# First output projection: groups 0 to 2 with tokens as output rows and a turn through DRAM, sums of squares moved into the next projection

## The reference, cut to what matters

```python
def pool_mixer(h, w_in, w_grp, scale, w_out):
    ...
    y = jnp.einsum('btgc,gcd->btgd', pooled, w_grp).reshape(B, T, BRANCH_W) * scale
    return (y * jax.nn.silu(g)) @ w_out          # the first output projection
...
    x = x + gate * y
    return rms_norm(x) * final_norm_g            # end of the first block
...
def gated_deltanet(h, w_in, ...):                # after another rms_norm of h
    proj = h @ w_in.astype(h.dtype)              # the projection called G_A below
    qkv = proj[..., :3 * A_INNER]
    a_in = proj[..., 4 * A_INNER:4 * A_INNER + A_HEADS]
    b_in = proj[..., 4 * A_INNER + A_HEADS:]
```

## Time and profile before

| what | value |
|---|---|
| median of 3 runs | 1334.66 us (1333.32 to 1334.88) |
| profiled execution, its own time | 1334.82 us |
| span of the profile | 1332.7 us |
| TensorE matmul busy | 1326.0 us (99%) |
| VectorE busy | 960.7 us (72%) |
| ScalarE busy | 732.5 us (55%) |
| DMA, mean over the span | 255 GB/s |
| first output projection begins | 247.55 us |
| first group of `G_A` begins, next group begins | 338.34 us, 365.21 us |

### The profile page before, as it was taken

How to read it: one execution, slowest core, us unless ns; L and a number is a source line. 1 busy time by engine, 2 the same in 40 slices (tenths; PEclk the granted TensorE clock), 3 DMA queues, 4 the chain that set the end, 5 groups by cost and what they waited for, 6 DMA issues and landing times.

```text
span 1332.7 us, 18992 instructions
## 1 busy us (share of the span) xinstructions
PE 1326.0 (99%) x6963; PEld 1109.1 (83%) x6963; DVE 960.7 (72%) x1279; ACT 732.5 (55%) x1091; POOL 196.8 (15%) x313
## 2 busy tenths in 40 slices
PE   9999999999999999999999999999999999999999
PEld 5445999988888888888888988888888888888887
DVE  4558999988779898999676668746666566666552
ACT  2213435456766657556688775465655646565431
POOL 0000012100001000032122200002234234232000
PEclk9999999999999999999999999999999999999999
DMA  9999989885676776599866676656879889789662
GB/s 383 394 416 371 353 345 408 299 279 181 202 248 207 239 226 222 182 294 293 222 181 198 201 236 224 194 186 205 260 236 270 261 271 283 217 278 262 179 197 83
DMA packets 90354, 339.36 MB, mean 255 GB/s; under 512 B 12368, under 2 KB 12768, under 8 KB 85792
## 3 DMA queue, kind: packets, MB, share of 16 engines
q1 hardware_dynamic: 67392, 261.30, 57.7%
q0 software_dynamic: 22880, 76.94, 19.0%
HBM read 310.91 MB, written 29.38 MB: 255 GB/s over the span
## 4 chain that ended last, share of the span: by engine, by line
PE 81%; DMA 12%; DVE 5%; issue 1%; ACT 1%; SPq 0%; POOL 0%; DVEq 0%; POOLq 0%
PE acc L905 19%; PE acc L848 14%; PE acc L849 14%; PE acc L850 14%; PE acc L909 10%; DMA mod_ring<-mod_w 7%; DMA raw<-weights 5%; PE misc L1174 2%; DVE w_lo L1903 1%; PE misc L905 1%; PE misc L1164 1%; DVE mod_ring L1873 1%; PE misc L1065 1%; DVE mod_late L1873 1%; DVE gate_ring L1873 1%
## 5 line engine op out<-in xcount | busy, mean ns | idle before, releaser
L1903 DVE TENSOR_TENSOR w_lo<-raw,w_hi 128x1024 fp32r<-128x1024 f32 x392 | 471.5, 1221 | 178.7 <-ACT w_hi L1339 173.1
L1339 ACT ACTIVATE w_hi<-raw 128x1024 fp32r<-128x1024 f32 x392 | 405.4, 1054 | 321.6 <-DMA raw<-weights 234.7
L848 PE MATMUL acc<-w_hi,b_op 128*128 128x512 f32 x704 | 277.1, 394 | 0.0
L849 PE MATMUL acc<-w_lo,b_op 128*128 128x512 f32 x704 | 274.3, 390 | 0.0
L850 PE MATMUL acc<-w_hi,b_op 128*128 128x512 f32 x704 | 274.3, 390 | 0.0
L905 PE MATMUL acc<-b_op,w_hi 128*128 128x512 f32 x640 | 162.1, 395 | 0.0
L850 PEld LDWEIGHTS acc<-w_hi,b_op 128*128 128x128 f32 x704 | 132.2, 188 | 27.5
L848 PEld LDWEIGHTS acc<-w_hi,b_op 128*128 128x128 f32 x704 | 132.4, 188 | 26.3
L849 PEld LDWEIGHTS acc<-w_lo,b_op 128*128 128x128 f32 x704 | 132.4, 188 | 26.1
L905 PEld LDWEIGHTS acc<-b_op,w_hi 128*128 128x128 f32 x640 | 115.2, 189 | 21.0 <-issue 0.2
L905 PE MATMUL acc<-a_op,w_hi 128*128 128x512 f32 x448 | 113.1, 394 | 0.3 <-DVE a_op L1913 0.3
(11 more groups left out here) (314 smaller groups left out, 2012.8 us busy)
## 6 DMA issues: line engine op xcount, KB each, us to landing
raw<-weights SPq DMA_DIRECT2D x392, 512.0 KB, 5.1
mod_ring<-mod_w SPq DMA_DIRECT2D x26, 1024.0 KB, 14.4
u_ring<-weights SPq DMA_DIRECT2D x32, 512.0 KB, 14.6
gate_ring<-weights POOLq DMA_DIRECT2D x30, 512.0 KB, 8.3
mod_late<-mod_w SPq DMA_DIRECT2D x6, 1024.0 KB, 6.4
head_d<-head POOLq DMA_DIRECT2D x32, 128.0 KB, 4.3
t<-head_d POOLq DMA_DIRECT2D x32, 128.0 KB, 5.9
z_d<-z POOLq DMA_DIRECT2D x28, 128.0 KB, 4.8
```

Of the source, the lines that this page charges most:

```text
L848: nc.tensor.matmul(to, xh[:, t], wh, start=kt == 0, stop=False)
L849: nc.tensor.matmul(to, xh[:, t], wl, start=False, stop=False)
L1339: nc.scalar.activation(w_hi[:, m.c % HL_SLOTS], raw[:, q.c % RAW_SLOTS], ACT.Copy).then_inc(own.up(s_hi), 1)
L1903: nc.vector.tensor_tensor(w_lo[:, slot], raw[:, q.c % RAW_SLOTS], w_hi[:, slot].bitcast(F32), ALU.subtract).then_inc(own.up(s_lo), 1)
```

## The change

Groups 0 to 2 of the first output projection are computed by token into three pairs of PSUM banks. ScalarE copies each to SBUF (`out_by_token`), VectorE transposes its blocks (`out_turned`), GpSimd turns it through DRAM, and VectorE adds the result, times the gate, to the residual in one step per group (`gated`, four instructions). Group 3 stays `joined`, in the plain order. VectorE's work there is written out anew: group 3's second half is added before the squares of group 2 are summed. `early_sums` moves from group 3 into the first group of `G_A`, behind its slab at position 3, and `last_sums` from position 4 to 5. Weights of the three groups are laid out on the host in the other slab form. Numbers of turns that other stages wait for are shifted by three.

```diff
-TURNS = tuple([("va", v) for v in range(4)] + [("za", 0), ("za", 1), ("za", 2)] +
+TURNS = tuple([("y", j) for j in range(3)] + [("va", v) for v in range(4)] + [("za", 0), ("za", 1), ("za", 2)] +
...
+        y_part = [vo[:, k:k + 4].rearrange("p k t -> p (k t)") for k in (8, 4, 8)]
+        y_32 = at("y_32", [P, 4 * T], F32, vo_at + 12288)
...
-            for j in (2, 3):
-                pool.wait_ge(s_gate, 29 + j)
-                x_again(j)
...
+            def out_turned(j):
+
+                n, through = turn_of("y", j), head_d[0] if j == 1 else z_d
+                pool.wait_ge(s_head_32, n)
+                to_dram(y_32[:], through, s_head_d)
+                if j == 0:
+                    for k in (2, 3):
+                        pool.wait_ge(s_gate, 29 + k)
+                        x_again(k)
+                pool.wait_ge(s_head_d, 64 * n)
+                from_dram(through, y_part[j], s_z_t)
...
-                pe.wait_ge(s_sums, 4)
+                pe.wait_ge(s_sums, 6)
                 partition_sums(t3, misc[:, 0:T], last=False)
-                pe.wait_ge(s_sums, 5)
+                pe.wait_ge(s_sums, 7)
                 partition_sums(t4, misc[:, 512:512 + T], last=False)
 
-            for j in range(4):
-                joined(G_WOUT + j, a_op, ready=None if j else lambda kt: O_H + kt // 4 + 1,
-                       fillers={6: early_sums} if j == 3 else None, order=PLAIN if j else SPLIT)
+            for j in range(3):
+                pe.wait_ge(s_free, j + 1)
+                group(None, slab_of(Num(G_WOUT + j)), pair_of_banks(j), 0, a_hi, a_lo, products=by_token,
+                      ready=None if j else lambda kt: O_H + kt // 4 + 1)
+            joined(G_WOUT + 3, a_op)
...
-            joined(G_A, b_op, ready=operand_b, fillers={4: last_sums, 6: decay_and_beta}, order=SPLIT)
+            joined(G_A, b_op, ready=operand_b, fillers={3: early_sums, 5: last_sums, 6: decay_and_beta}, order=SPLIT)
...
-            hi_parts(Num(N_WOUT + 9), 6)
+            def out_by_token(j):
+
+                act.wait_ge(s_used, slab_of(Num(G_WOUT + j + 1)).c)
+                if j == 2:
+                    act.wait_ge(s_x1, 1)
+                to = y_part[j].rearrange("p (m a c) -> p a m c", m=GM, a=2)
+                src = acc[:, j] if j < 2 else misc[:, 0:2 * GC]
+                for half in range(2):
+                    of = src[:, half * GC:(half + 1) * GC].rearrange("p (m c) -> p m c", m=GM)
+                    nc.scalar.activation(to[:, half], of, ACT.Copy).then_inc(own.up(s_zs if half else s_act), 1)
+
+            hi_parts(Num(N_WOUT + 9), 3)
+            out_by_token(0)
+            hi_parts(Num(N_WOUT + 12), 3 + SLABS - 1)
...
+                if j < 2:
+                    out_by_token(j + 1)
+                    hi_parts(slab_of(Num(G_WOUT + j)) + (AHEAD + 7), 1)
                 act.wait_ge(s_x1, j + 1)
...
+            def out_turned(j):
+
+                n = turn_of("y", j)
+                dve.wait_ge(s_zs, n)
+                for _ in range(2):
+                    dve.sem_inc(own.also(s_free), 1)
+                if j:
+                    dve.wait_ge(s_head_d, 64 * (n - 1))
+                nc.vector.transpose(y_32[:], y_part[j]).then_inc(own.up(s_head_32), 1)
+
+            def gated(j):
+
+                dve.wait_ge(s_z_t, 64 * turn_of("y", j))
+                dve.wait_ge(s_x_again[j], 16)
...
+            gated(1)
+            out_turned(2)
+            lo_parts(Num(N_WOUT + 30), 1)
+            operand_of(1)
+            squares_added(1)
+            lo_parts(Num(N_WOUT + 31), 4)
+            gated_half(3, 0)
+            lo_parts(Num(N_WOUT + 35), 2)
+            gated(2)
+            operand_of(2)
+            gated_half(3, 1)
+            squares_added(2)
+            folded(t3, s_sums)
+            folded(t4, s_sums)
+            lo_parts(Num(N_WOUT + 37), 1)
+            operand_of(3)
+            dve.wait_ge(s_sq, 4 + 16)
+            folded(t0, s_fold)
+            dve.wait_ge(s_sq, 4 + 20)
+            folded(t1, s_fold)
...
+            lo_parts(Num(N_WOUT + 38), 5)
+            dve.wait_ge(s_root, 2)
+            dve.wait_ge(s_stat, 3)
+            add(r2[:], misc[:, 512:512 + T], r1, ALU.mult)
```

More of the change, by code:

```diff
@@ L649, in _, with to_dram, from_dram @@
                         x_again(j)
-            for j in (2, 3):
-                pool.wait_ge(s_gate, 29 + j)
-                x_again(j)
+            def to_dram(tile, through, written):
+                for a in range(4):
+                    rows = tile[32 * a:32 * a + 32].rearrange("p (n c) -> p n c", c=P)
+                    pool.dma_start(through[:, :, a], rows).then_inc(written, 16)
+            def from_dram(through, tile, done):
+                for b in range(4):
+                    of = through.rearrange("x n a c -> x (n a) c")[:, :, 32 * b:32 * b + 32]
+                    pool.dma_start(tile[32 * b:32 * b + 32].rearrange("p (k t) -> p k t", t=32), of
+                                   ).then_inc(done, 16)
+            def out_turned(j):
[8 more added lines that the diff above has]
+                from_dram(through, y_part[j], s_z_t)
+            out_turned(0)
             pool.dma_start(head_rows[:], rows_d.to_broadcast([P, 2 * P])).then_inc(s_rows, 16)
@@ L704, in _ @@
                 query_parts(j)
-            def to_dram(tile, through, written):
-                for a in range(4):
-                    rows = tile[32 * a:32 * a + 32].rearrange("p (n c) -> p n c", c=P)
-                    pool.dma_start(through[:, :, a], rows).then_inc(written, 16)
-            def from_dram(through, tile, done):
-                for b in range(4):
-                    of = through.rearrange("x n a c -> x (n a) c")[:, :, 32 * b:32 * b + 32]
-                    pool.dma_start(tile[32 * b:32 * b + 32].rearrange("p (k t) -> p k t", t=32), of
-                                   ).then_inc(done, 16)
             def first_gate_turned(j):
@@ L2080, in gated_half @@
                         nc.vector.scalar_tensor_tensor(
-                            out=xres[:, kt], in0=sums_of(u)[:, (2 * m + part) * T:(2 * m + part + 1) * T],
+                            out=xres[:, kt], in0=acc[:, u % 2, (2 * m + part) * T:(2 * m + part + 1) * T],
                             scalar=modv[:, 2 * KT + kt:2 * KT + kt + 1], in1=xres[:, kt], op0=ALU.mult, op1=ALU.add
@@ L2085, in gated_half @@
                 dve.sem_inc(own.also(s_free), 1)
+            def out_turned(j):
[9 more added lines that the diff above has]
+                dve.wait_ge(s_x_again[j], 16)
+                for m in range(GM):
+                    kt = 4 * j + m
+                    nc.vector.scalar_tensor_tensor(
+                        out=xres[:, kt], in0=tiles(y_part[j])[:, m], scalar=modv[:, 2 * KT + kt:2 * KT + kt + 1],
+                        in1=xres[:, kt], op0=ALU.mult, op1=ALU.add
+                            ).then_inc(own.up(s_x1 if m == GM - 1 else s_dve), 1)
@@ new lines, in squares_added @@
+            def squares_added(j):
+                dve.wait_ge(s_sq, 4 + 5 * j + 1)
+                add(t3[:], t3[:], t0[:, 0:4 * T], done=s_sums)
+                dve.wait_ge(s_sq, 4 + 5 * j + 5)
+                add(t4[:], t4[:], t1[:, 0:4 * T], done=s_sums)
+            gated(0)
+            out_turned(1)
+            lo_parts(Num(N_WOUT + 22), 1)
+            operand_of(0)
+            lo_parts(Num(N_WOUT + 23), 7)
+            gated(1)
+            out_turned(2)
+            lo_parts(Num(N_WOUT + 30), 1)
@@ new lines, in _ @@
+            folded(t1, s_fold)
+            dve.wait_ge(s_ab_hi, 1)
+            nc.vector.tensor_tensor(ab_lo, ab_raw[:].rearrange("p (k c) -> p k c", k=KT),
+                                    ab_hi.bitcast(F32), ALU.subtract).then_inc(own.up(s_ab_lo), 1)
+            lo_parts(Num(N_WOUT + 38), 5)
+            dve.wait_ge(s_root, 2)
+            dve.wait_ge(s_stat, 3)
+            add(r2[:], misc[:, 512:512 + T], r1, ALU.mult)
+            dve.wait_ge(*own.last())
+            add(r2[:], r2[:], r1, ALU.mult, done=s_var2)
@@ L2136, in _ @@
+            dve.wait_ge(s_root, 3)
+            add(r2[:], r2[:], r1, ALU.mult)
+            dve.wait_ge(*own.last())
+            lo_parts(Num(N_WOUT + 43), 3)
+            evicted_half(G_A, 0, r2[:])
+            lo_parts(Num(N_WOUT + 46), 1)
             dve.wait_ge(s_ab_part, 2)
```

83 lines of the change are left out of this document (23 added, 60 removed).

## The result

| | before | after |
|---|---|---|
| median | 1334.77 us (4 runs, 1333.32 to 1335.51) | 1345.08 us (4 runs, 1343.96 to 1347.72) |
| profiled execution, own time | 1334.82 us | 1343.96 us |
| span of the profile | 1332.7 us | 1342.2 us |

The changed kernel takes 1.0082 times the time of before (95% interval 1.0067 to 1.0097): it is slower by 0.8%, some 10 us. 1336.1 was forecast, with a range to 1340.8; the measured time lies above it.

What follows compares the result with a forecast made beforehand. TensorE was taken to bound the kernel. The next group starts 1.1 us later, plus 0.3 for `ab_c`: 1.4 on 1334.8 gives 1336.2, less 0.16 to the median: 1336.1 us. Range 1333.6 to 1340.8, likeliest case 1335.1 to 1337.1.

Steps and rivals of the forecast that it cites:

- TensorE's own time: Groups 0 to 2: 2.72 us a slab instead of 2.79, no start wait; 2.3 us gained at most.
- The rival in which by token saves nothing: Slabs of groups 0 to 2: only columns count, so TensorE and walk are 1.7 later; 1337.8 us, chance 0.06.
- The place and the mechanism of the wait: Next group's start: W+42's late load delays r1's logarithm on ScalarE, so VectorE frees the accumulator at 366.2, not before 362.9.
- the walk: VectorE's steps timed in order from group 2's end at 312.85 to the accumulator's freeing at 366.2, 1 us either way.
- From r1 to the end of the freeing step: Behind the first root: 8.8 us as in the kernel before, since the order in between is the same.
- The rival in which the roots wait for TensorE only: W+42 comes in time and r1 waits only for TensorE's sums: 1334.4, or 1332.4 if all is hidden; chance 0.20.
- These lie beside TensorE as long as weight slabs stay ahead ... DMA queues have room: Added copies and transposes in the output projection stay hidden; W+23 ready some 9 us before TensorE wants it.
- The rival of the late turn: Group 2's turn lands late, so `gated(2)` and all behind come 4.0 later: 1340.1, up to 1343; chance 0.24.
- quiet 12.3 and busy 19.8: Duration in us of group 2's turn through DRAM in a quiet or busy stretch; 15.4 available, quiet judged nearer.
- a wait of 3.4 us: TensorE at the next group's start, waiting for VectorE's freeing step: starts at 366.3 instead of 362.9.
- the upper end 1343: Highest time, in us, of the case in which group 2's turn and the second turn are both late.
- the wait for `ab_c`: One slab into the next group, TensorE waits another 0.3 us for `ab_c` from VectorE.

Runs made afterwards that it cites:

- version 11: Changed kernel reordered so TensorE's needs don't stand behind weight loads, late residual loads behind the turns' reads, decays' product one slab later: 1331.76 us, ratio 0.9988 to before.
- experiment 10: Changed kernel with the turns' writes to DRAM cut to an eighth of their bytes, reads in full: 1344.53 us, ratio 1.0086 to the kernel before.
- experiment 12: Changed kernel with only the two late residual loads put back behind the reads of turns 0 and 1: 1344.65 us, ratio 1.0087 to the kernel before.
- experiment 6: Changed kernel with the turns' reads in whole rows of 4 KB instead of 128 byte pieces: 1344.29 us, ratio 1.0072 to the kernel before.
- experiment 4: Changed kernel with group 2's squares again summed and folded ahead of group 3's second half: 1346.79 us, ratio 1.0091 to the kernel before.
- experiment 8: Changed kernel reordered so TensorE's needs don't stand behind weight loads, late residual loads moved behind the first two turns' reads: 1334.91 us, ratio 1.0002 to before.
- experiment 3: Changed kernel with the three turns' writes and reads both cut to an eighth of their bytes: 1336.08 us, ratio 1.0014 to the kernel before.
- experiment 1: Changed kernel with slab W+42's high and low parts moved behind the work on the two roots: 1339.8 us, ratio 1.0041 to the kernel before.
- experiment 5: Changed kernel with W+42 and followers behind work TensorE waits for, accumulator freed before the second root, early sums one slab later: 1337.98 us, ratio 1.0029 to before.

## Why the prediction was wrong, and where it was right

**TensorE's own time: right.** 2.72 us a slab, no start wait, 2.3 us less in all; the trace of version 11 shows 2.1 of them, and its time fits (0.4 to 2.8 us). The rival in which by token saves nothing falls with it. The Trainium skill (TensorE: Matmul & The Clock Gate, Back-to-back issue gap), by the formula that it gives there for an isolated matmul, would have given 0.24 us for the 24 slabs; the trace of after has 24 x (2.79 - 2.72) = 1.7.

**The place and the mechanism of the wait: right.** W+42 ahead of the roots, r1 behind it, the accumulator late. With the turns' bytes small the kernel follows the walk to within 2 us: `gated(2)` at 329.0 (330.9 forecast), W+42's high part at 351.5 (352.9), a wait of 3.1 (3.4), and 1336.08 us (1336.1). That the two times agree is luck: the next group began 1.4 us sooner than in the walk, and the slow slab behind its wait, which the sum did not have, cost 1.4. From r1 to the end of the freeing step it took 372.56 - 363.74 = 8.8 us after the change, as forecast from the rows. The rival in which the roots wait for TensorE only did not come in: W+42 was 6.7 us too late for it after the change (the logarithm began at 361.5, its sums were ready at 354.8), and 1.3 us too late even with small turns.

**The step that failed: "These lie beside TensorE as long as weight slabs stay ahead ... DMA queues have room".** That row is of 315 to 332, 0.46 busy, and covers only the third turn. Turns 0 and 1 fall into stretches that were 0.83 and 0.64 busy already, and I left these out. The walk then took VectorE's order as if every low part found its slab ("now follow at once"). After the change they waited 19.3 us in all. So the transpose of group 2 was forecast at 314.3 and came at 318.3, 4.0 later; turn 2 landed 17.1 us after its start (319.96 to 337.05), where there was room for 15.4, with the second low part ahead of it as late. `gated(2)` came 6.1 late, and W+42's high part 6.3 (359.2 for 352.9). My question was whether slabs stay ahead of TensorE. They did. The one to ask was whether they stay ahead of VectorE's place in its own order. (A slip of the walk, four low parts from 320.9 to 325.8 where they end at 325.5, changes nothing: VectorE then waits for W+35 and W+36 anyway.)

**The rival of the late turn: it is the case that came in, with its size short.** Between its quiet 12.3 and busy 19.8 the truth was 17.1, and I leaned to the quiet one by a DMA share that left out what the turn adds: the stretch went from 0.60 to 0.83. The rival gave 4 to 7 us on the forecast; 6.3 is inside. But it let turn 2 be late by itself, and experiment 10 shows `gated(1)` late behind a slab with its turn landed. By the Trainium skill (DMA: Bandwidth & Descriptors, Issuing engines are not separate DMA queues) transfers of all issuers share the same 16 engines; the loads at 7.2 us beside the reads and 4.7 without agree.

**A term that was missing: the clock.** The forecast had a wait of 3.4 us cost 3.4. It costs 1.4 to 2.5 more: the slab behind took 4.3, 4.5, 4.5 and 5.0 us, where 2.9 is the rule, behind waits of 3.1, 3.4, 2.0 and 8.5, and over all traces 4.3 to 5.4. The price does not follow the length: 4.3 and 5.4 us stand behind waits of 8.6 (experiments 12 and 6), 5.4 also behind one of 3.3 (experiment 4). It makes the upper end 1343 into 1345. In the kernel before no wait of TensorE in this stage is longer than 0.3 us, so no row there showed it; but I named a wait as my forecast and should have put a bound on what follows a wait.

**Early sums: small miss.** That they stood behind late squares (+1.7 us in the tally) I had not listed; it cost nothing on top, since the freeing step was what TensorE waited for next, and it was set by ScalarE.

**The range.** It ended at 1340.8 because the late turn's upper half and a slow clock were outside. With the walk's delay of 6.3 and the slab's 2.1 the same sum gives 1336.2 + 6.3 + 2.1 - 0.3 (the wait for `ab_c`, which did not come up) = 1344.3 for a measured 1344.0 of the profiled execution.

## What to carry to other kernels

When a change adds traffic, read the DMA share of the stretch in which each added transfer falls, and walk the consumers in their written order: a late load harms whatever stands behind its use on that engine, long before the matrix engine lacks data. A forecast wait of the matrix engine should carry a bound for the slower work behind it. And when a change frees time on the critical engine but loses it to order, the order can be mended: here nearly all of the engine's own 2.3 us came out once nothing that could be late stood ahead of what it waits for.

## What the runs showed of the hardware

- The granted clock falls when TensorE stands idle for 2 to 8.5 us in a stretch of full work, and stays down through the slab behind: 0.67 over the wait of 8.5 and 0.55 behind it; 0.62 to 0.66 over the slab behind waits of 2.0, 3.1 and 3.4 us (experiments 8, 3 and 1), with 0.99 to 1.00 over those waits themselves. Over the slab behind waits of 3.3 and 8.6 us in experiments 4 and 6 it was 0.50 throughout. TensorE kept busy: 1.00, and the slab 3.1 us. Behind waits of 1.3 to 1.5 us (experiments 1, 4 and 5) it stayed at 1.00 and the slab took 2.9.
- 512 KB weight loads beside the third turn (316 to 336 us): 7.2 us to landing; beside small reads, 4.7. With the writes small and the reads in full they took 6.2.
- Reads in rows of 4 KB landed a little sooner than in short pieces (6.1 for 7.5 us in the last stretch) and slowed the weights as much.
